# Second attention of a two-model kernel: transposes, copies and value products of a unit stand one step further behind its exponentials

## The chip, the cores and the metric

The kernel runs on one core of a Trainium2 chip. The metric is the device time of one execution in microseconds, and the text gives its median over runs. The five engines of the core each run their own instructions in order and wait for one another by semaphores: TensorE (PE, its weight loads as PEld), VectorE (DVE), ScalarE (ACT), GpSimd (POOL) and SyncE (SP, which issues transfers).

## The reference, cut to what matters

A first block (feed-forward, a mixer with a recurrence and an attention, feed-forward) is followed by a second block of two layers. The change is in the windowed attention of the second block's last layer: 16 query heads of 64 columns over 4 key heads, 512 positions in 4 blocks of 128. Each block sees its own and both neighbouring blocks (with a mask) and 256 context positions, and each head has a sink that only enters the sum.

```python
def block(bidx):
    qb = lax.dynamic_slice_in_dim(qg, start, ATT_BLOCK, axis=1)
    kb = lax.dynamic_slice_in_dim(kp, start, 3 * ATT_BLOCK, axis=1)
    vb = lax.dynamic_slice_in_dim(vp, start, 3 * ATT_BLOCK, axis=1)
    s_loc = jnp.einsum("bqkgd,bskd->bkgqs", qb, kb)
    s_loc = jnp.where(mask, s_loc, NEG_INF)
    s_ctx = jnp.einsum("bqkgd,bskd->bkgqs", qb, kc)
    p = jax.nn.softmax(jnp.concatenate([s_loc, s_ctx, s_sink], axis=-1), axis=-1)[..., :-1]
    return (jnp.einsum("bkgqs,bskd->bqkgd", p_loc, vb)
            + jnp.einsum("bkgqs,bskd->bqkgd", p_ctx, vc))
yl = jnp.moveaxis(ob, 0, 1).reshape(B, L, Q_DIM) @ w_o
```

## The kernel before

The attention is cut into 32 units (`UNITS`), each a pair of heads at one block of 128 queries, and four units make a group, which has one product with the values. `unit` gives a unit's number of key blocks: 5 (3 local and 2 of the context) for the middle two of the four query blocks, called **wide** here, and 4 for the first and the last, called **narrow**. Units 0 to 7 and 24 to 31 are narrow, 8 to 23 are wide, so of the groups 0 to 7 the groups 2 to 5 are wide.

A unit goes through these steps. The short names are used in all that follows:

- **S**, `att_scores`, PE (L694, L699): four products, local scores into banks 2 and 3, context scores into banks 0 and 1. It waits until DVE has read the scores of the unit before (`s_evac`).
- **stats**, `att_stats`, DVE (L1786 to L1794): sink column, masked copy, context copy (`s_evac` here), then the row extremum (`max_ready`).
- **E**, `att_exps`, ACT (L1242): two exponentials with their row sums, then `exp_ready`.
- **T** and **T'**, `att_turns`, PE (L715): 8 transposes into banks 4 and 5 for the block groups 0 and 1, and for a wide unit 2 more, T', for block group 2. T waits for `exp_ready` of its unit; every block group also waits until the one two before it has been copied out (`t_evac`), since there are two banks.
- **C** and **C'**, `att_copies`, ACT (L1255): the copies of those banks to `pT2`.
- For a group: **recip** on DVE (L1799), **rows** on PE (L725), the **rows copy** on ACT (L1261, `rec_copied`), **spread** on PE (L732, waits for the rows copy), the **spread copy** on ACT (L1268), **V** on PE (`att_values`, L747, 20 products of 512 columns for a wide group and 16 for a narrow one), and the **output** on DVE (`att_outputs`, L1806).

No scheduler sets the order. Each engine has a loop over U written out by hand, and what stands in a row there is run in that row; a wait holds everything behind it on that engine. One pass of such a loop is called step U here, and steps are named by U modulo 4 where that suffices: step 2 is any U with remainder 2. Before, the loops of PE and ACT are:

```
PE:  T(U-2)   S(U)     T'(U-2)  [U%4==1: rows]  [U%4==2: V, spread]
ACT: C(U-2)   E(U-1)   C'(U-2)  [U%4==2: rows copy]  [U%4==3: spread copy]
DVE: stats(U) [U%4==0: recip]   [U%4==3: output]
```

`sm2`, which holds the scores and then the exponentials, has room for four units, `pT2` for two groups. After the loops all engines but SP meet at a barrier (`phase.end`), and the projection `wo` (L524) follows.

Of the kernel before, what the change touches and what calls it, by code (L numbers as in the profile page):

```python
# [115 lines left out]
def program(nc, d):  # L116
    ctx = ExitStack()
    with ctx:
# [48 lines left out]
        def const(name):  # L167
            a, n = CONST_AT[name]
            return consts[:, a:a + n]
# [188 lines left out]
        UNITS = 4 * KT  # L358

        def unit(second, U):  # L360


            n, kv, i = U // 8, U // 4 % 2, U % 4
            lo, hi = max(n - 1, 0), (min(n + 1, LT - 1) if second else n) + 1
            return 4 * kv + i, n, kv, lo, hi, (lo - n + 1) * P, hi - lo + (2 if second else 0)

        def turned(second, U, g=0):

            return (UNITS if second else 0) + sum(-(-2 * unit(second, u)[6] // 4) for u in range(U)) + g
# [138 lines left out]
        def _(pe):  # L508
# [178 lines left out]
            def att_scores(second, U):  # L687
                x, n, kv, lo, hi, _, per = unit(second, U)
                q, k = (qt2, kt2) if second else (qk1, kt1)
                if U or second:  # L690
                    pe.wait_ge(s_evac, (UNITS if second else 0) + U)
                for s in range(2):
                    h = slice(64 * s, 64 * s + 64)
                    mm = nc.tensor.matmul(bank[2 + s][:, 0:(hi - lo) * P], q[h, x, n * P:(n + 1) * P], k[h, kv, lo * P:hi * P],  # L694
                                          start=True, stop=True)
                if second:
                    for s in range(2):
                        h = slice(64 * s, 64 * s + 64)
                        mm = nc.tensor.matmul(bank[s][:, 0:C], q[h, x, n * P:(n + 1) * P], k[h, kv, S:SC], start=True, stop=True)  # L699
                mm.then_inc(s_full, 1)  # L700

            def att_turns(second, U, gs):

                per = unit(second, U)[6]
                sm = sm2 if second else sm1
                for g in gs:
                    if 4 * g >= 2 * per:
                        continue
                    at = turned(second, U, g)
                    if g == 0:  # L710
                        pe.wait_ge(exp_ready, (UNITS if second else 0) + U + 1)
                    if at > 1:
                        pe.wait_ge(t_evac, at - 1)
                    for y in range(4 * g, min(4 * g + 4, 2 * per)):
                        tr = nc.tensor.transpose(bank[4 + at % 2][:, (y % 4) * P:(y % 4 + 1) * P],  # L715
                                                 sm[:, U % (4 if second else 3), y // per, (y % per) * P:(y % per + 1) * P], ident)
                    tr.then_inc(t_full, 1)

            def att_rows(second, G):

                N = (UNITS // 4 if second else 0) + G
                pe.wait_ge(rec_ready, N + 1)
                if N:
                    pe.wait_ge(rec_copied, 2 * N)
                nc.tensor.matmul(bank[7][0:8, 0:P], rec8[G % 2], ident, start=True, stop=True).then_inc(rec_full, 1)  # L725

            def att_spread(second, G):

                N = (UNITS // 4 if second else 0) + G
                pe.wait_ge(rec_copied, 2 * N + 1)  # L730
                for i in range(4):
                    mm = nc.tensor.matmul(bank[7][:, i * P:(i + 1) * P], const("head")[0:8, i * P:(i + 1) * P], rec_rows, start=True, stop=True)  # L732
                mm.then_inc(rec_full, 1)

            def att_values(second, G):

                U = 4 * G + 3
                x, n, kv, lo, hi, _, per = unit(second, U)
                pT, v = (pT2, v2) if second else (pT1, v1)
                G0 = UNITS // 4 if second else 0  # L740
                pe.wait_ge(t_evac, turned(second, U + 1))
                if G0 + G:
                    pe.wait_ge(o_evac, G0 + G)
                for y in range(per):
                    tile = lo + y if y < hi - lo else LT + y - (hi - lo)
                    for s in range(2):
                        mm = nc.tensor.matmul(bank[6][64 * s:64 * s + 64, :], v[:, tile, (2 * kv + s) * HD:(2 * kv + s + 1) * HD],  # L747
                                              pT[G % 2][:, s * per + y, :, :].rearrange("p i q -> p (i q)"), start=(y == 0), stop=(y == per - 1))
                mm.then_inc(o_full, 1)
# [323 lines left out]
                    pe.wait_ge(rope_free, 10 + ROTATED.index(x - ROPE_LAG) + 1)  # L1073
                    nc.tensor.matmul(bank[6][:, :], const("swap2"), HEAD_TILES[x - ROPE_LAG], start=True, stop=True).then_inc(rope_full, 1)
            phase.end()
            for U in range(UNITS + 3):
                if 0 <= U - 2 < UNITS:
                    att_turns(True, U - 2, (0, 1))
                if U < UNITS:
                    att_scores(True, U)  # L1080
                if 0 <= U - 2 < UNITS:
                    att_turns(True, U - 2, (2,))
                if U > 4 and U % 4 == 1:
                    att_rows(True, U // 4 - 1)
                if U > 4 and U % 4 == 2:
                    att_values(True, U // 4 - 1)
                    att_spread(True, U // 4 - 1)
            phase.end()
            dense("wo", 2, lambda j, k: f[:, k, :])
            phase.end()  # L1090
# [5 lines left out]
        def _(act):  # L1096
# [138 lines left out]
            def att_exps(second, U):  # L1235

                w = unit(second, U)[6] * P + 1
                sm = (sm2 if second else sm1)[:, U % (4 if second else 3), :, :]
                st = small[:, 16 * (U % 4):16 * (U % 4) + 16]
                act.wait_ge(max_ready, (UNITS if second else 0) + U + 1)  # L1240
                for s in range(2):
                    nc.scalar.activation(sm[:, s, 0:w], sm[:, s, 0:w], ACT.Exp, bias=st[:, 4 + s:5 + s], scale=-1.0,  # L1242
                                         accum_out=sums8[U // 4 % 2][:, 2 * (U % 4) + s:2 * (U % 4) + s + 1])
                act.drain().then_inc(exp_ready, 1)

            def att_copies(second, U, gs):
                per = unit(second, U)[6]
                pT = (pT2 if second else pT1)[U // 4 % 2]
                for g in gs:
                    w = min(4, 2 * per - 4 * g)  # L1250
                    if w <= 0:
                        continue
                    at = turned(second, U, g)
                    act.wait_ge(t_full, at + 1)
                    nc.scalar.activation(pT[:, 4 * g:4 * g + w, U % 4, :], bank[4 + at % 2][:, 0:w * P].rearrange("p (b q) -> p b q", b=w),  # L1255
                                         ACT.Copy).then_inc(t_evac, 1)

            def att_rows(second, G):
                N = (UNITS // 4 if second else 0) + G
                act.wait_ge(rec_full, 2 * N + 1)  # L1260
                nc.scalar.activation(rec_rows, bank[7][0:8, 0:P], ACT.Copy).then_inc(rec_copied, 1)  # L1261
# [324 lines left out]
                                     scale=1.0 / HD).then_inc(qstd_ready, 1)  # L1586
            phase.end()
            for U in range(UNITS + 4):
                if 0 <= U - 2 < UNITS:
                    att_copies(True, U - 2, (0, 1))  # L1590
                if 0 <= U - 1 < UNITS:
                    att_exps(True, U - 1)
                if 0 <= U - 2 < UNITS:
                    att_copies(True, U - 2, (2,))
                if U > 4 and U % 4 == 2:
                    att_rows(True, U // 4 - 1)
                if U > 4 and U % 4 == 3:
                    att_spread(True, U // 4 - 1)
# [8 lines left out]
        def _(dve):  # L1607
# [193 lines left out]
            def att_outputs(second, G):  # L1801
                x, n = unit(second, 4 * G)[:2]
                N = (UNITS // 4 if second else 0) + G
                dve.wait_ge(o_full, N + 1)
                dve.wait_ge(rec_copied, 2 * N + 2)
                nc.vector.tensor_tensor((f if second else qk1)[:, x:x + 4, n * P:(n + 1) * P], bank[6][:, :].rearrange("p (i q) -> p i q", i=4),  # L1806
                                        rec2 if second else rec1, ALU.mult).then_inc(o_evac, 1)
# [430 lines left out]
            phase.end()  # L2238
            nc.vector.tensor_scalar(minus_sinks, vec("sinks2"), -1.0, None, ALU.mult)
            dve.drain()  # L2240
            for U in range(UNITS + 4):
                if U < UNITS:
                    att_stats(True, U)
                if U > 0 and U % 4 == 0 and U <= UNITS:
                    att_recips(True, U // 4 - 1)
                if U > 4 and U % 4 == 3:
                    att_outputs(True, U // 4 - 1)
            phase.end()
            gated_add("wo", 1, 2, False)
            phase.end()  # L2250
# [236 lines left out]
```

## Time and profile before

| | |
|---|---|
| time before, median of 3 runs | 3304.15 us (3304.03 to 3306.55) |
| profiled execution, its own time | 3304.57 us |
| its span in the trace | 3302.8 us |
| PE matmul busy, share of the span | 2824.1 us, 86% |
| DVE busy | 1287.5 us, 39% |
| ACT busy | 803.8 us, 24% |
| the second attention, first S to the first product of `wo` | 2474.66 to 2631.30 us |
| busy in 2540 to 2560 us of it | PE 17.41, DVE 13.07, ACT 13.23 of 20 us |
| granted TensorE clock, mean of the execution | 0.928 |

The stage that is changed is 156.6 us long, 4.7% of the execution. Most of the rest is feed-forward, projections and mixture of experts, in which the change moves nothing. The share of a stage says which engine is fullest there; which wait ends last there is read from the rows of the timeline, given below.

### The profile page before, as it was taken

To read this page: it belongs to the slowest core of one execution; us is meant where nothing else is said; L and a number is where in the kernel's file an instruction comes from. 1 tells how busy PE (TensorE), PEld (TensorE's weight loads), DVE (VectorE), ACT (ScalarE), POOL (GpSimd) and SP (SyncE) were. 2 spreads that over 40 slices of the span, in tenths; PEclk is the share of its full clock that TensorE was granted. 3 is DMA by queue.
4 is the path that set the end of the run, shared out by engine and by line. 5 is a ranking of instruction groups with operands and counts; after the bars stand their busy time and mean duration, and the time that the engine had idled before them with its cause. 6 is when DMAs were issued, how large, how long until landed. Compare 5 with 4: busy or idle time off the path is not lost. (4 is left out here: it accounts for less than half of the span.)

```text
span 3302.8 us, 34854 instructions
## 1 busy us (share of the span) xinstructions
PE 2824.1 (86%) x12512; PEld 1823.7 (55%) x12512; DVE 1287.5 (39%) x1978; ACT 803.8 (24%) x1338; POOL 366.9 (11%) x484
## 2 busy tenths in 40 slices
PE   6999998999989998798868888885778887888886
PEld 4888766767768886685643333333544433333333
DVE  4776676454476755303221111113386421111112
ACT  3233235453333222222210000001326520000000
POOL 0111000000000111322101111111400001111110
PEclk9999999999999999799869898997889997999998
DMA  4666521112235665110229999995100036999997
GB/s 169 210 222 219 197 77 64 67 66 85 98 137 192 222 235 187 43 59 15 96 107 398 402 401 399 403 400 221 50 27 1 1 123 248 401 400 397 400 405 297
DMA packets 117476, 672.08 MB, mean 203 GB/s; under 512 B 16399, under 2 KB 20879, under 8 KB 51857
## 3 DMA queue, kind: packets, MB, share of 16 engines
q1 hardware_dynamic: 77456, 542.63, 42.4%
q0 software_dynamic: 33600, 104.90, 9.2%
q10 hardware_dynamic: 6336, 23.50, 2.0%
q8 instruction: 46, 0.75, 0.1%
q14 instruction: 38, 0.30, 0.0%
HBM read 672.78 MB, written 24.38 MB: 211 GB/s over the span
## 5 line engine op out<-in xcount | busy, mean ns | idle before, releaser
L823 PE MATMUL bank<-big 128*64 128x512 f32 x1040 | 479.0, 605 | 110.3 <-DMA big<-in_w 108.5
L826 PE MATMUL bank<-big 128*64 128x512 f32 x1040 | 481.4, 607 | 0.0
L1962 DVE TENSOR_TENSOR big<-big,bank 64x512 f32<-64x512 f32 x65 | 44.9, 692 | 916.3 <-ACT big L1303 916.3
L823 PEld LDWEIGHTS bank<-big 128*64 128x64 f32 x1040 | 137.7, 139 | 420.5 <-issue 418.4
L838 PE MATMUL bank<-big 128*64 128x512 f32 x1040 | 284.5, 698 | 44.4 <-DVE big L1966 44.4
L1670 DVE SCALAR_TENSOR_TENSOR tabs<-tabs,tmp 128x1024 f32<-128x1024 f32 x160 | 193.1, 1222 | 181.1 <-DMA tabs<-in_wm 180.5
L2325 POOL DMA_DIRECT2D tabs<-in_wm x160 | 85.0, 532 | 1193.0 <-DVE tabs L1670 753.6
L536 PE MATMUL bank<-act_low 128*128 128x512 f32 (+1 forms) x480 | 166.3, 363 | 48.5 <-POOL u_split L2310 25.5
L838 PEld LDWEIGHTS bank<-big 128*64 128x64 f32 x1040 | 82.6, 158 | 197.8 <-issue 196.5
L1157 ACT ACTIVATE w_high<-slot 128x1024 fp32r<-128x1024 f32 (+1 forms) x134 | 136.6, 1040 | 220.3 <-DMA slot<-in_w 94.8
L1303 ACT ACTIVATE big<-bank 64x512 f32<-64x512 f32 x65 | 38.3, 589 | 539.4 <-PE bank L823 539.4
L542 PE MATMUL bank<-u_split,w_low 128*128 128x512 f32 x656 | 162.3, 389 | 3.5 <-DVE w_low L1623 3.5
L930 PE MATMUL bank<-u_split,w_high 128*128 128x512 f32 x400 | 158.6, 396 | 0.0
L930 PE MATMUL bank<-u_low,w_high 128*128 128x512 f32 x368 | 155.2, 422 | 0.2 <-ACT w_high L1157 0.2
L1309 ACT ACTIVATE big<-bank 128x512 f32<-128x512 f32 x65 | 38.8, 597 | 457.2 <-PE bank L838 457.2
L542 PEld LDWEIGHTS bank<-u_split,w_low 128*128 128x128 f32 x656 | 123.0, 188 | 29.9 <-DVE w_low L1623 4.3
L826 PEld LDWEIGHTS bank<-big 128*64 128x64 f32 x1040 | 137.6, 139 | 0.0
L536 PE MATMUL bank<-u_split,w_high 128*128 128x512 f32 x320 | 127.1, 397 | 8.2 <-ACT w_high L1157 8.2
L536 PEld LDWEIGHTS bank<-act_low 128*128 128x128 f32 x480 | 93.6, 195 | 70.5 <-issue 24.3
L536 PE MATMUL bank<-u_split 128*128 128x512 f32 x336 | 131.6, 392 | 0.0
L536 PE MATMUL bank<-u_low,u_split 128*128 128x512 f32 x336 | 130.7, 389 | 0.0
L536 PE MATMUL bank<-u_low,w_high 128*128 128x512 f32 x320 | 126.5, 395 | 0.0
(353 smaller groups left out, 5195.1 us busy)
## 6 DMA issues: line engine op xcount, KB each, us to landing
big<-in_w SPq DMA_DIRECT2D x402, 1024.0 KB
slot<-in_w SPq DMA_DIRECT2D x100, 1024.0 KB, 4.9
tabs<-in_wm POOLq DMA_DIRECT2D x160, 512.0 KB, 4.8
slot<-in_wd SPq DMA_DIRECT2D x16, 1408.0 KB, 6.5
big<-yb ACTq DMA_DIRECT2D x20, 512.0 KB, 4.8
rows<-big ACTq DMA_DIRECT2D x10, 512.0 KB, 2.6
lat<-in_x SPq DMA_DIRECT2D x1, 2048.0 KB, 9.9
out<-lat SPq DMA_DIRECT2D x4, 512.0 KB, 3.2
```

What stands on the lines that cost most here:

```text
L536: mm = nc.tensor.matmul(out, piece[0][k], part_of[k], start=flag, stop=False)
L542: mm = nc.tensor.matmul(out, piece[1][k], high[k], start=False, stop=(last and k == n - 1))
L823: ga = nc.tensor.matmul(bank[0][lo, :], xT[:, 4 * c + k, :], wslot[c][:, k * EF:(k + 1) * EF], **flags)
L826: mm = nc.tensor.matmul(bank[0][hi, :], xT[:, 4 * c + k, :], wslot[2 + c][:, k * EF:(k + 1) * EF], **flags)
L838: mm = nc.tensor.matmul(bank[4][half, :], hT[:, 2 * c + k, :], wslot[4 + c][:, k * D + n * 512:k * D + (n + 1) * 512], start=(c == 0 and k ...
L930: mm = nc.tensor.matmul(out, wh[n // 2], (lo, hi)[n % 2][n // 2], start=(n == 0), stop=False)
L1157: nc.scalar.activation(rings[ring][:, 0:at.stop - at.start], slot[s][:, at], ACT.Copy).then_inc(wh_ready, 1)
L1303: nc.scalar.activation(hsil[MB:2 * MB, :], bank[0][0:MB, :], ACT.Silu).then_inc(q["sg_ready"], 1)
L1309: nc.scalar.activation(ysb, bank[4][:, :], ACT.Copy).then_inc(q["y_ready"], 1)
L1670: nc.vector.scalar_tensor_tensor(mslot[m % 2], mslot[m % 2], 1.0, crow, ALU.mult, ALU.mult, accum_out=modf[:, idx:idx + 1]).then_inc(mod_d ...
L1962: nc.vector.tensor_tensor(hmul[MB:2 * MB, :], hsil[MB:2 * MB, :], bank[0][MB:2 * MB, :], ALU.mult).then_inc(q["h_ready"], 1)
L2325: pool.dma_start(mslot[m % 2], d["wm"][(MOD_OF[1] + MOD_OF[2])[m] // 2]).then_inc(mod_load[m % 2], 16)
```

## The change

Every place of T, T', C and C' moves from unit U-2 to unit U-3 within the loops of PE and ACT; S, stats and E stay. V moves from step 2 to step 3, while spread stays in step 2, now with nothing between it and T'. The output moves from step 3 to the next step 0, behind recip. The loops of PE and DVE are one pass longer.

```diff
-            for U in range(UNITS + 3):
-                if 0 <= U - 2 < UNITS:
-                    att_turns(True, U - 2, (0, 1))
+            for U in range(UNITS + 4):
+                if 0 <= U - 3 < UNITS:
+                    att_turns(True, U - 3, (0, 1))
                 if U < UNITS:
                     att_scores(True, U)
-                if 0 <= U - 2 < UNITS:
-                    att_turns(True, U - 2, (2,))
+                if 0 <= U - 3 < UNITS:
+                    att_turns(True, U - 3, (2,))
                 if U > 4 and U % 4 == 1:
                     att_rows(True, U // 4 - 1)
                 if U > 4 and U % 4 == 2:
+                    att_spread(True, U // 4 - 1)
+                if U > 4 and U % 4 == 3:
                     att_values(True, U // 4 - 1)
-                    att_spread(True, U // 4 - 1)
...
-                if 0 <= U - 2 < UNITS:
-                    att_copies(True, U - 2, (0, 1))
+                if 0 <= U - 3 < UNITS:
+                    att_copies(True, U - 3, (0, 1))
                 if 0 <= U - 1 < UNITS:
                     att_exps(True, U - 1)
-                if 0 <= U - 2 < UNITS:
-                    att_copies(True, U - 2, (2,))
+                if 0 <= U - 3 < UNITS:
+                    att_copies(True, U - 3, (2,))
...
-            for U in range(UNITS + 4):
+            for U in range(UNITS + 5):
                 if U < UNITS:
                     att_stats(True, U)
                 if U > 0 and U % 4 == 0 and U <= UNITS:
                     att_recips(True, U // 4 - 1)
-                if U > 4 and U % 4 == 3:
-                    att_outputs(True, U // 4 - 1)
+                if U > 4 and U % 4 == 0:
+                    att_outputs(True, U // 4 - 2)
```

The first piece is PE's loop, the second ACT's, the third DVE's.

On PE, steps 29 to 31 and the start of what follows (narrow units), before: L725 is rows, L715 is T, L694 and L699 are S, L747 is V and L732 is spread.

```order
L725 MATMUL bank<-consts,rs 8x128
L715 MATMUL bank<-consts,big 128x128 x8
L694 MATMUL bank_3<-big 128x256 x2
L699 MATMUL bank_1<-big 128x256 x2
L747 MATMUL bank<-big 64x512 x8
L732 MATMUL bank<-rs,consts 128x128 x4
L715 MATMUL bank<-consts,big 128x128 x8
L694 MATMUL bank_3<-big 128x256 x2
L699 MATMUL bank_1<-big 128x256 x2
```

The same place of the changed kernel:

```order
L725 MATMUL bank<-consts,rs 8x128
L715 MATMUL bank<-consts,big 128x128 x8
L694 MATMUL bank_3<-big 128x256 x2
L699 MATMUL bank_1<-big 128x256 x2
L732 MATMUL bank<-rs,consts 128x128 x4
L715 MATMUL bank<-consts,big 128x128 x8
L694 MATMUL bank_3<-big 128x256 x2
L699 MATMUL bank_1<-big 128x256 x2
L747 MATMUL bank<-big 64x512 x8
```

V has gone from in front of spread to behind the next step's T and S, and spread now follows S directly.

On ACT, two wide steps around the rows copy, in the changed kernel (all line numbers are one higher there): L1256 are C' (128x2x128) and C (128x4x128), L1243 is E, L1262 the rows copy, L1269 the spread copy.

```order
L1256 ACTIVATE big<-bank 128x4x128 x2
L1243 ACTIVATE big,rs<-big,small 128x641 x2
L1256 ACTIVATE big<-bank 128x2x128
L1262 ACTIVATE rs<-bank 8x128
L1256 ACTIVATE big<-bank 128x4x128 x2
L1243 ACTIVATE big,rs<-big,small 128x641 x2
L1256 ACTIVATE big<-bank 128x2x128
L1269 ACTIVATE tmp<-bank 128x512
```

The order of kinds is that of before. What moved is which unit C and C' belong to; the rows copy still stands behind E and C' of step 2.

On DVE, around the output of a wide group, before: L1787, L1790 and L1794 are the rest of stats, L1806 is the output and L1786 begins the next stats.

```order
L1787 SCALAR_TENSOR_TENSOR big<-bank_3,consts 128x2x384
L1790 TENSOR_SCALAR big<-bank_1 128x2x256
L1794 TENSOR_REDUCE small<-big 128x2
L1806 TENSOR_TENSOR ar_f<-bank,tmp 128x4x128
L1786 COPY big<-small 128x2
```

In the changed kernel, around the output of such a group:

```order
L1791 TENSOR_SCALAR big<-bank_1 128x2x256
L1795 TENSOR_REDUCE small<-big 128x2
L1800 RECIPROCAL rs<-rs 128x8
L1807 TENSOR_TENSOR ar_f<-bank,tmp 128x4x128
L1787 COPY big<-small 128x2
```

The output has come to stand behind the reciprocal (L1800) of the next group, in step 0.

## Rows read from the trace of the kernel before

**Rows 1.** Waits in 2470:2640: engine, line waited for; us in total, times, longest

```profile
PE bank L715 <- ACTq L1244: 25.0, 24, 2.2
```

**Rows 2.** Timeline, PE, one wide group: start us, us, line, operation [idle before]

```profile
2545.01 1.12 PE L715 MATMUL bank<-consts,big 128*128 128x128 f32 x8 [0.73 <-ACTq L1244]
...
2553.77 0.92 PE L694 MATMUL bank<-big 64*128 64x384 f32 x4
...
2555.41 4.51 PE L747 MATMUL bank<-big 128*64 128x512 f32 x20
...
2559.85 1.15 PE L732 MATMUL bank<-rs,consts 8*128 8x128 f32 x8
...
2560.94 1.09 PE L715 MATMUL bank<-consts,big 128*128 128x128 f32 x8
...
2561.96 0.92 PE L694 MATMUL bank<-big 64*128 64x384 f32 x4
...
2564.41 1.12 PE L715 MATMUL bank<-consts,big 128*128 128x128 f32 x8 [0.73 <-ACTq L1244]
```

**Rows 3.** Timeline, ACT, the same group: rows copy, E, C', spread copy

```profile
2556.81 0.25 ACT L1261 ACTIVATE rs<-bank 8x128 f32<-8x128 f32 x1
...
2562.60 0.83 ACT L1242 ACTIVATE big<-big,small 128x641 f32<-128x641 f32 x1
...
2564.43 0.39 ACT L1255 ACTIVATE big<-bank 128x256 f32<-128x256 f32 x1
...
2564.71 0.59 ACT L1268 ACTIVATE tmp<-bank 128x512 f32<-128x512 f32 x1
```

**Rows 4.** Timeline, DVE, the same group: sink column, reduce, output, next sink column

```profile
2563.36 0.17 DVE L1786 COPY big<-small 128x2 f32<-128x2 f32 x1 [4.99 <-PE bank L699]
...
2565.07 1.49 DVE L1794 TENSOR_REDUCE small<-big 128x2 f32<-128x1282 f32 x1
...
2566.48 0.68 DVE L1806 TENSOR_TENSOR ar_f<-bank,tmp 128x512 f32<-128x512 f32 x1
...
2567.08 0.16 DVE L1786 COPY big<-small 128x2 f32<-128x2 f32 x1
```

**Rows 5.** Timeline, PE, one narrow group

```profile
2601.95 1.09 PE L715 MATMUL bank<-consts,big 128*128 128x128 f32 x8 [1.10 <-ACTq L1244]
...
2609.49 0.70 PE L694 MATMUL bank<-big 64*128 64x256 f32 x4
...
2610.55 3.65 PE L747 MATMUL bank<-big 128*64 128x512 f32 x16
...
2618.47 1.09 PE L715 MATMUL bank<-consts,big 128*128 128x128 f32 x8 [1.10 <-ACTq L1244]
```

**Rows 6.** Groups by shape in 2490:2628: busy us, mean ns, idle before

```profile
L1787 DVE SCALAR_TENSOR_TENSOR big<-bank,consts 128x768 f32<-128x768 f32 x16 | 15.2, 952 | 0.0
...
L1794 DVE TENSOR_REDUCE small<-big 128x2 f32<-128x1026 f32 x13 | 15.9, 1222 | 1.2
...
L1787 DVE SCALAR_TENSOR_TENSOR big<-bank,consts 128x512 f32<-128x512 f32 x13 | 8.9, 684 | 0.0
...
L1242 ACT ACTIVATE big<-big,small 128x513 f32<-128x513 f32 x27 | 19.2, 718 | 0.0
```

**Rows 7.** Timeline, the start of the stage: context copy of unit 1, S of unit 2

```profile
2481.01 0.68 DVE L1790 TENSOR_SCALAR big<-bank 128x512 f32<-128x512 f32 x1
...
2484.33 1.23 PE L694 MATMUL bank<-big 64*128 64x256 f32 x4
```

**Rows 8.** Timeline, PE, the end of the stage and the first of wo

```profile
2621.72 1.82 PE L715 MATMUL bank<-consts,big 128*128 128x128 f32 x8 [2.16 <-ACTq L1244]
...
2624.23 4.18 PE L747 MATMUL bank<-big 128*64 128x512 f32 x16 [0.16 <-ACT big L1255]
...
2631.30 10.97 PE L524 MATMUL bank<-ar_f,slot 128*128 128x512 f32 x21 [1.80 <-POOLq L355]
```

**Rows 9.** Windows: us, busy PE, PEld, DVE, ACT, POOL (count); granted clock; DMA share, GB/s

```profile
2632.50:2635.00 2.50, 2.50 (x5) 0.95 (x4) 0.00 (x0) 0.00 (x0) 0.00 (x0) 0.50 0.02 7
```

## The prediction

> **What bounds the kernel now.** I read the waits of the stage first, then the timeline of one group, and follow each engine from row to row. PE is the fullest engine of the stage, yet it waits 24 times, 25.0 us in all, for the exponentials of the unit that it is to transpose; DVE in turn waits for scores, 4.99 us behind a V [rows 1, 4]. A wide group takes 19.4 us: T starts at 2545.01, and the T four steps on at 2564.41 [rows 2]. In a step without V, T starts at 2560.94 and the next at 2564.41, 3.47 us later [rows 2]. The reader is to see that this is a closed loop: T at 2560.94, its copies, E at 2562.60, the next T at 2564.41 [rows 2, 3]. Between them ACT copies unit U-2, then does E of unit U-1, and PE needs exactly this E for its next T. The step with V is the other part: V takes from 2555.41 to 2559.85, 4.44 us, spread 1.09, and DVE then sits 4.99 us without scores [rows 2, 4]. Per wide group PE waits a few tenths to over a microsecond in each of the other three steps; 25.0 us is all that can be won if nothing else comes in.
>
> **What the change removes.** T of a unit now comes one step later, so its E was done a step before: T's wait for E goes away. The upper bound of this is the 25.0 us [rows 1]. The longer loop through DVE (S, stats, E, T, S) now spans three units and binds nothing. No operation is added or dropped but one pass of the loops; no transfer is in the stage's loops.
>
> **What is late next: the second half of T.** T's second four transposes reuse the bank of T' of the unit before, so they wait for C', and C' stands behind E on ACT. In the walk below this costs 0.7 us in step 1 and 1.0 in step 2 of a wide group (C' starts 1.83 behind E [rows 3]), between 0 and 1.0 in general, and it lies off the path that sets the end, since stats of unit 0 decides both steps. The Trainium skill (Perfetto Trace Analysis, Identifying Performance Opportunities) reads bubbles that repeat as a sign of too few buffers. It would put the remaining loss down to the two transpose banks; by my walk the sum is the same with or without that wait, and no row of before shows the wait.
>
> **What is late next: spread.** Spread waits for the rows copy on ACT. That copy stands in step 2 behind E and C'. Before, V lay in front of spread: the rows copy began at 2556.81, V had begun at 2555.41 and ran to 2559.85, so V hid the wait whole [rows 2, 3]. Now spread stands right behind T', and everything behind it on PE (T, S and V of step 3) waits with it.
>
> I walk one wide group from V to V, always along what comes last:
> - V to the T of step 0: 4.44; T to S: 1.02 (2560.94 to 2561.96) [rows 2]
> - S of unit 0 to the start of its stats: 1.40 (to 2563.36); to the reduce: 1.71 (to 2565.07) [rows 2, 4]
> - the reduce to the next DVE operation, now recip: 1.41 (2565.07 to 2566.48) [rows 4]; recip itself adds 0.1 (an estimate, between 0 and 0.2, since short operations overlap); the output, which now stands here, 0.60 (2566.48 to 2567.08) [rows 4]
> - stats of unit 1: 1.71 to its reduce, 1.49 for it, then E of unit 1: 3.20 [rows 4]
> - E to C' 1.83, C' to the next on ACT, now the rows copy, 0.28 (2562.60, 2564.43, 2564.71) [rows 3]
> - the rows copy 0.25 [rows 3] and its release 0.05 (an estimate): 0.30
> - spread 1.09, T to S 1.02, S and T' 1.64 (2553.77 to 2555.41), then V again [rows 2]
>
> Sum: 4.44 + 1.02 + 1.40 + 1.71 + 1.41 + 0.1 + 0.60 + 3.20 + 1.83 + 0.28 + 0.30 + 1.09 + 1.02 + 1.64 = 20.04 us, against 19.40: **0.65 slower**. PE would be ready for spread 1.8 us earlier (S of unit 2 can start about 8.5 behind the T of step 0, spread 1.64 later at 10.1; the rows copy is there at 11.9).
>
> The narrow group by the same walk: V shorter by 0.86 (4.51 less 3.65), S by 0.22 (0.92 less 0.70), S and T' to V 1.06 for 1.64 (2609.49 to 2610.55), two masked copies shorter by 0.27 each (952 and 684 ns), two reduces by 0.27 each (1.49 and 1222 ns), E by 0.21 (two of 0.83 and 718 ns), no C' 0.28 [rows 2 to 6]. 20.04 less 3.23 is 16.8, against 16.5 for one group (2601.95 to 2618.47 is 16.52 [rows 5]): **0.3 slower**. Its wait for the rows copy is longer, 2.1 us, since PE has less to do.
>
> **Sum over the stage, clock aside.** Eight groups go round. Three are wide throughout: 3 x 0.65 = +1.9. One is narrow throughout, +0.3. The first has no output in its step 0 and so is 0.6 shorter than a narrow one: -0.3. Two mix wide and narrow units, between 0.1 and 0.7 each: +0.8 together. The start: S of unit 2 no longer waits for the first T; it can start when unit 1's scores are read, 2481.01 + 0.68 = 2481.69, against 2484.33 [rows 7]: -2.6. The end: one step more, T without S, but spread and its copy now lie ahead of V or under it. From the T of step 32 to wo it was 2618.47 to 2631.30, 12.8 us [rows 5, 8]; the same steps in the new order come to about 11.7, and wo may start at the full clock: between -1.1 and -2.7, I take -1.5. Sum: 1.9 + 0.3 - 0.3 + 0.8 - 2.6 - 1.5 = **-1.4 us**.
>
> **The clock.** The granted clock is at its full level (2.4 GHz) in all the middle of the stage. At the end the T at 2621.72 takes 1.82 us where T takes 1.09: after 2.16 us of idle PE the clock was at its lower level (1.2 GHz) [rows 5, 8]. The first products of wo, after 1.80 us idle, ran low too, with a granted clock of 0.50 in 2632.5 to 2635 [rows 8, 9]. The V behind the first of these took 4.18 against 3.65 [rows 5, 8], so one fall costs 0.73 + 0.53 and a few tenths for the S between: 1.5 us. Idle of 1.10 in a step did not lower it [rows 5]. The new wait for the rows copy is 2.1 us in the groups with narrow E, three of them, with 0.4 idle shortly before, and 1.7 to 1.8 in wide ones. The first is as long as the one that lowered the clock, the second just short of the other. I take three falls, +4.5; the ends are none, 0, and eight, +12. With it the forecast is -1.4 + 4.5 = **+3.1 us**. The profiled execution's own time is 3304.57, so 3307.7 on it; it lies 0.4 above the median of 3304.15, and on the median I say **3307.3**.
>
> **The rivals.**
> - *Slower, by the clock.* If the wide groups' waits of 1.7 to 1.8 us lower the clock as well, spread, T, S and V run low behind each wait, and all of them lie on the path. Eight falls: -1.4 + 12 = +10.6, 3314.8. It decides at five falls (+6.1), about where a difference can be told. For it: 1.80 did it before wo. Against: in a wide group T' and the split T leave PE busier just before.
> - *Quicker, the wait is covered.* If the rows copy were there when PE comes to spread, the wide walk would end with S of unit 2 at 8.5, then 1.64 + 1.09 + 1.02 + 1.64 + 4.44: 18.3, 1.1 less than before, and a narrow group 14.7, 1.8 less. Three wide, two mixed at 1.5, three narrow: -3.3 - 3.0 - 5.4, with start and end -4.1: -15.8, 3288. For it speaks only that the waited-for E goes; against it that the rows copy stood behind E and C' at 2556.81, 1.4 us behind the point at which spread would now be issued [rows 2, 3]. The Trainium skill (Perfetto Trace Analysis, Identifying the Most-Contended Engine) takes weight-load time, not matmul time, for how near TensorE is to its limit; by that PE has room and most of the 25.0 us could come back, 3279 at best. The rows speak against it: from start to start PE's own work fills all but about 2.6 of 19.4 us of a wide group.
> - *The clock never falls.* The waits for the rows copy stay too short, and start and end weigh against the eight groups: -1.4, 3302.8.
>
> **How the numbers follow.** Forecast (the wait for the rows copy shows, two to four falls) 0.47; no or one fall 0.18, 3302.8 to 3304; five or more falls 0.24, 3310 to 3317; wait covered 0.08, 3288; something on PE that no row shows, 0.03 to either side. A measurement of this kernel can tell about 0.2%, 6.6 us. Faster by more than that (below 3297.5): the covered case and the odd one, 0.10. Slower (above 3310.8): 0.24 of falls less the part that stays below, plus the odd one, 0.23. Within: 0.67. The range leaves out the covered case (0.08), the odd ones and the top of the falls: 3300 to 3315.
>
> **What would show it.** A wait of PE at L733 (spread) for ACT's rows copy (L1262), 8 times, 1.7 to 2.2 us each, some 15 us in all, where before had none. PE's wait for exponentials at T falls from 25.0 us to under 5, and waits at the second half of T for C' come up in the wide groups. A wide group of 20.0 us and a narrow one of 16.8. DVE's wait for scores about as before. Spreads of 1.5 to 2 us instead of 1.15, and T of 1.8, where the clock fell. The forecast is wrong if spread shows no wait, if a wide group is below 19 us, or if the clock is low behind each wide group's wait.

## The result, and the profile after

The changed kernel takes 3320.1 us (median of 6 runs, 3318.7 to 3320.9), the kernel before 3304.1 in 6 runs beside it: a ratio of 1.0045, 95% interval 1.0033 to 1.0057. It is 0.45% or 15 us slower by the ratio, which goes by all runs; the two medians lie 16 us apart. The forecast was 3307.3 with a range of 3300 to 3315, so the time lies outside the range, on the side of the rival that goes by the clock. Another set of runs gave 1.0039 (1.0025 to 1.0053).

The profiled execution after has a span of 3317.7 us, 14.9 more than before. From the first S of the second attention to the first product of `wo` it takes 169.3 us (2475.18 to 2644.50) against 156.6. `wo` itself is 1.7 us shorter, since it now starts at the full clock. What is ahead of the stage differs by 0.5 us and what is behind `wo` by 3.4, in work that the change leaves alone.

The waits of PE in the stage, in the changed kernel (engine, line waited for; us in total, times, longest; lines of PE's helpers keep their numbers, so spread is L732, where the prediction wrote L733, and T is L715; lines behind the loops are one higher than before, so L1262 is the rows copy, L1256 C and C', L1791 the context copy of stats):

```profile
PE bank L732 <- ACT rs L1262: 13.5, 8, 2.4
PE bank L715 <- ACT big L1256: 6.4, 9, 1.0
PE bank L694 <- DVE big L1791: 6.0, 8, 1.5
...
PE bank L725 <- DVE rs L1800: 1.6, 3, 1.0
```

The 25.0 us that PE waited for exponentials [rows 1] are gone without a rest. In their place stand 13.5 us at spread, eight times, 6.4 us at the second half of T, 6.0 for the reading of scores and 1.6 at rows: 27.5 us, only 2.5 more than those 25.0. That alone is no 15 us.

One wide group in which the clock stays up, PE (start us, us, line, operation, idle before):

```profile
2551.21 1.09 PE L715 MATMUL bank<-consts,big 128*128 128x128 f32 x8
...
2555.14 0.66 PE L715 MATMUL bank<-consts,big 128*128 128x128 f32 x4 [0.76 <-ACT big L1256]
...
2563.06 1.15 PE L732 MATMUL bank<-rs,consts 8*128 8x128 f32 x8 [1.62 <-ACT rs L1262]
...
2566.82 4.51 PE L747 MATMUL bank<-big 128*64 128x512 f32 x20
...
2571.26 1.09 PE L715 MATMUL bank<-consts,big 128*128 128x128 f32 x8
```

and in the same group ACT, with the weight loads of spread (PEld):

```profile
2562.48 0.38 ACT L1256 ACTIVATE big<-bank 128x256 f32<-128x256 f32 x1
2562.76 0.25 ACT L1262 ACTIVATE rs<-bank 8x128 f32<-8x128 f32 x1
2563.06 0.96 PEld L732 LDWEIGHTS bank<-rs,consts 8*128 8x128 f32 x8 [1.85 <-ACT rs L1262]
```

From T to T it is 20.05 us, where the walk of the prediction gave 20.04 and before had 19.40 [rows 2]. The rows copy begins 0.28 behind C' and spread 0.30 behind its begin, to the hundredth what was summed up. DVE goes from the reduce of unit 0 through recip and output to the stats of unit 1 without waiting:

```profile
2555.34 1.49 DVE L1795 TENSOR_REDUCE small<-big 128x2 f32<-128x1282 f32 x1
2556.75 0.19 DVE L1800 RECIPROCAL rs<-rs 128x8 f32<-128x8 f32 x1
2556.86 0.64 DVE L1807 TENSOR_TENSOR ar_f<-bank,tmp 128x512 f32<-128x512 f32 x1
2557.41 0.16 DVE L1787 COPY big<-small 128x2 f32<-128x2 f32 x1
```

PE had the scores of unit 1 ready at 2557.07, ahead of the stats at 2557.41, though the second half of T at 2555.14 had waited 0.76 us for C': that wait is off the path, as the walk had it.

Now the narrow group at the end, PE:

```profile
2611.22 1.09 PE L715 MATMUL bank<-consts,big 128*128 128x128 f32 x8
...
2618.09 0.70 PE L694 MATMUL bank<-big 64*128 64x256 f32 x4 [0.41 <-DVE big L1791]
...
2621.32 2.07 PE L732 MATMUL bank<-rs,consts 8*128 8x128 f32 x8 [2.10 <-ACT rs L1262]
2623.32 1.97 PE L715 MATMUL bank<-consts,big 128*128 128x128 f32 x8
2625.22 1.23 PE L694 MATMUL bank<-big 64*128 64x256 f32 x4
...
2627.22 3.87 PE L747 MATMUL bank<-big 128*64 128x512 f32 x16
2631.03 1.09 PE L715 MATMUL bank<-consts,big 128*128 128x128 f32 x8
```

Up to spread it follows the walk. Then spread takes 2.00 us to the next T instead of 1.09, T 1.90 to S instead of 1.02, S 2.00 to V instead of 1.06: 2.7 us lost in the three, and 0.2 in V. The group takes 19.81 us against 16.52 before [rows 5] and 16.8 in the walk.

The granted clock in stretches of the changed kernel (us; busy PE, PEld, DVE, ACT, POOL; granted clock; DMA share, GB/s):

```profile
2518.70:2525.30 6.60, 5.78 (x24) 4.53 (x24) 1.66 (x2) 3.04 (x8) 0.00 (x0) 0.50 0.00 0
2542.30:2545.70 3.40, 3.40 (x15) 2.51 (x15) 0.40 (x1) 1.70 (x3) 0.00 (x0) 0.51 0.02 5
2556.00:2572.00 16.00, 13.59 (x83) 7.24 (x82) 10.74 (x15) 9.52 (x23) 0.00 (x0) 1.00 0.00 1
...
2621.00:2627.40 6.40, 6.08 (x26) 4.70 (x28) 1.00 (x2) 2.87 (x7) 0.00 (x0) 0.50 0.00 0
```

A stretch at the lower level (1.2 GHz) is called a fall of the clock here. Five of the eight waits at spread have one that begins in the wait or within 2 us behind it, 3.4 us long at two of them and 6.8 at three, and a sixth fall, of 3.4 us, begins just ahead of the last V. From 14 us into the stage on, before had a single one, of 3.4 us, in the T at 2621.72 [rows 8].

### The profile page after: what moved, and what is told of

It is laid out like the page before. It is cut to its first block and busy times, and to the rows that moved or that the text cites. A ratio compares the mean times of both kernels' runs of the same rounds, so it can differ in the third digit from the quotient of the medians.

```text
span 3317.7 us, 34854 instructions
## 1 busy us (share of the span) xinstructions
PE 2838.2 (86%) x12512; PEld 1832.1 (55%) x12512; DVE 1287.0 (39%) x1978; ACT 803.9 (24%) x1338; POOL 366.2 (11%) x484
```

## The experiments

Theory A: the wait for the rows copy, uncovered at spread, costs a little by itself and most through the clock that falls behind it. Theory B: the deeper lag costs, by its additional step and the split T. The table sums up all runs; each ratio is to the kernel before in the same set of runs. "Wide" is the time from S of unit 16 to S of unit 20, "narrow" from S of unit 4 to S of unit 8 (ahead of the first output), "low" the time at the lower clock in the stage, its first 16 us left out. Stage, wide, narrow and low come from one profiled execution of each kernel.

| kernel | ratio (95% interval) | stage, us | wide | narrow | low |
|---|---|---|---|---|---|
| before | 1 | 156.6 | 19.40 | 16.58 | 3.4 |
| changed | 1.0045 (1.0033 to 1.0057) | 169.3 | 20.05 | 19.43 | 31 |
| changed, again | 1.0039 (1.0025 to 1.0053) | 173.2 | 20.05 | 19.45 | 37 |
| e1, spread behind V | 0.9968 (0.9954 to 0.9982) | 148.3 | 19.47 | 14.70 | 0.8 |
| e2, rows copy first | 0.9948 (0.9928 to 0.9968) | 143.9 | 18.39 | 14.57 | 3.4 |
| e3, lag of two, spread uncovered | 1.0031 (1.0018 to 1.0043) | 172.3 | 23.20 | 16.86 | 31 |
| e4, four fillers | 1.0029 (1.0020 to 1.0039) | 169.5 | 21.94 | 17.78 | 0 |
| e5, two fillers | 0.9994 (0.9985 to 1.0004) | 156.8 | 20.22 | 16.26 | 0 |
| e6, e2 and C' first | 0.9966 (0.9952 to 0.9979) | 143.0 | 17.72 | 14.57 | 6.8 |
| e7, e2 and output in step 1 | 0.9957 (0.9944 to 0.9971) | 143.5 | 18.37 | 14.57 | 3.4 |
| e8, e3 and rows copy first | 0.9980 (0.9971 to 0.9990) | 150.3 | 18.38 | 15.58 | 6.8 |
| e9, e6 and e7 | 0.9956 (0.9942 to 0.9970) | 140.7 | 17.58 | 14.57 | 3.4 |
| e10, e9 and fillers at the end | 0.9947 (0.9934 to 0.9959) | 139.1 | 17.58 | 14.57 | 0 |

Times of the whole kernel scatter by some 5 us up and down in these sets (before: 3299.6 to 3312.0). In the traces much of that lies outside the stage: its first S comes between 2469.0 and 2477.7 us, and from the first product of `wo` to the end it takes 670.7 to 679.1. So the stage's own length shows more than the ratios do, as long as the falls in it are looked at too: the changed kernel's two executions differ by 3.9 us there, by their falls. (In the second, two records of the first S are missing; its start is set from the spacing of the next ones.)

**e1, spread covered by V again.**

```diff
-                if U > 4 and U % 4 == 2:
-                    att_spread(True, U // 4 - 1)
                 if U > 4 and U % 4 == 3:
                     att_values(True, U // 4 - 1)
+                    att_spread(True, U // 4 - 1)
```

> The changed kernel with spread moved behind V in step 3; the lag of three stays. Theory A (the uncovered wait for the rows copy, and the clock that falls behind it, make the change slower): PE waits no more at spread, the clock falls no more in the middle of the stage, a wide group takes about 19.4 us (V 4.44 and spread 1.09 as before, but the second half of T waits for C'), a narrow one about 15.2, the stage about 149 us against 156.6 before: 3296 us. Theory B (the deeper lag costs by itself, through one more step and the split T): the time stays near the changed kernel's 3320.

Waits of PE in the stage in e1:

```profile
PE bank L715 <- ACT big L1255: 10.2, 13, 1.0
PE bank L694 <- DVE big L1790: 7.6, 11, 1.5
```

No wait at spread, no fall of the clock but 0.8 us at the very end, a wide group of 19.47 us and a stage of 148.3: theory A's numbers (19.4 and 149); a narrow group takes 14.70 where 15.2 was expected. B falls: with the lag of three in full, the kernel is 0.3% faster than before. In wide groups the lag gains nothing this way; what PE no longer waits for E, it waits for C' (10.2 us).

**e2, the rows copy ahead of E.**

```diff
+                if U > 4 and U % 4 == 2:
+                    att_rows(True, U // 4 - 1)
                 if 0 <= U - 1 < UNITS:
                     att_exps(True, U - 1)
                 if 0 <= U - 3 < UNITS:
                     att_copies(True, U - 3, (2,))
-                if U > 4 and U % 4 == 2:
-                    att_rows(True, U // 4 - 1)
```

> The changed kernel with the rows copy of ACT moved ahead of E in step 2; PE's order is untouched. Theory A: spread finds the rows copy done, a wide group takes 18.3 us and a narrow one 14.7, no falls of the clock, stage about 142 us: 3290 us. Theory B: only the 13.5 us of waits at spread go at best, the falls stay: 3306 or more.

One wide group of e2, PE:

```profile
2547.28 0.44 PE L715 MATMUL bank<-consts,big 128*128 128x128 f32 x2
2547.64 1.15 PE L732 MATMUL bank<-rs,consts 8*128 8x128 f32 x8
2548.73 1.12 PE L715 MATMUL bank<-consts,big 128*128 128x128 f32 x8
...
2551.42 4.51 PE L747 MATMUL bank<-big 128*64 128x512 f32 x20
2555.86 1.09 PE L715 MATMUL bank<-consts,big 128*128 128x128 f32 x8
```

Spread follows T' by 0.36 us, without a wait, and PE runs from there through V without a gap. 18.39 us a wide group (18.3 expected), 14.57 a narrow one (14.7). "No falls" did not come true: one of 3.4 us is left in the last V, and the stage takes 143.9 us for 142. One ACT operation of 0.25 us, moved ahead of E, turns 0.45% slower into 0.52% faster. This is the rival "the wait is covered" of the prediction, made true.

**e3, the uncovered spread without the lag.** The kernel before, with V, spread and output where the change has them, T and C left at U-2:

```diff
                 if U > 4 and U % 4 == 2:
-                    att_values(True, U // 4 - 1)
                     att_spread(True, U // 4 - 1)
+                if U > 4 and U % 4 == 3:
+                    att_values(True, U // 4 - 1)
...
-                if U > 4 and U % 4 == 3:
-                    att_outputs(True, U // 4 - 1)
+                if U > 4 and U % 4 == 0:
+                    att_outputs(True, U // 4 - 2)
```

> The kernel before (lag of two) with only V, spread and the output placed as in the change: spread right behind T' in step 2, V in step 3, output in step 0. Theory A: spread waits 1.4 to 1.5 us for the rows copy in every group, a wide group takes 20.0 us and a narrow one 16.9; 3305 without a fall of the clock, up to 3315 with a fall in each narrow group. Theory B: placing spread there is harmless at any lag, 3304.

Its waits, and one low stretch of a wide group:

```profile
PE bank L715 <- ACTq L1245: 18.4, 17, 2.2
PE bank L732 <- ACT rs L1262: 11.2, 8, 1.6
```

```profile
2562.40:2569.00 6.60, 6.60 (x27) 4.27 (x27) 1.85 (x4) 3.20 (x8) 0.00 (x0) 0.51 0.00 0
```

It is slow without any deeper lag, by 0.31%, with 11.2 us of waits at spread and 31 us at the lower clock. The mechanism of A is confirmed. By the ratio the 10 us lie within what was expected (up to 11 with falls), but the profiled execution is among the slower ones and its stage is 15.7 us longer than before's: I had expected falls in narrow groups only, and all three wide groups have one (21.6, 23.2 and 21.7 us for a walk of 20.0), after waits of 1.6 us at most, while the first group, after a wait of 1.44, has none.

**e4 and e5, work in place of the wait.** Products of constants into the idle bank 6 ahead of each spread, four in e4 and two in e5. Each shows as two records in the trace, as every product here but the transposes does: the x20 of a wide V are 10 products of the program, the x16 of a narrow one 8. The edit of e5:

```diff
                 if U > 4 and U % 4 == 2:
+                    N = UNITS // 4 + U // 4 - 1
+                    pe.wait_ge(o_evac, N)
+                    for _ in range(2):
+                        nc.tensor.matmul(bank[6][0:64, :], consts[:, 0:64], consts[:, 0:512], start=True, stop=True)
                     att_spread(True, U // 4 - 1)
```

> The changed kernel with four products of 512 columns of constants into the idle bank 6 just ahead of each spread (1.7 us of PE work in the place of the wait; results unused). Theory A in its clock part: the granted clock stays at its full level through the stage, the spreads are 1.15 us again, and the 12 us that I read as lost to the clock come back: 3308 us, though PE does 14 us more work. If the falls are a side effect and the waits alone cost: 3320 or more.

> As e4_fillers, with two products in place of four: e4's four took 3.6 us ahead of each spread, longer than the wait that they replace (1.6 to 2.4 us), so its time held both effects; two take 1.8 us (results unused). If the falls of the clock make up the rest of the slowdown, no fall is left in the stage, a wide group stays at 20.05 us, a narrow one at 17, the stage takes 157 us against 169.3 of the changed kernel and the time equals before's, ratio 1.000. If the waits alone cost, it stays 0.3% or more above.

The narrow group of e5 that answers to the one shown of the changed kernel, PE (L1089 are the fillers):

```profile
2608.91 1.93 PE L1089 MATMUL bank<-consts 128*64 128x512 f32 x4
2611.08 1.15 PE L732 MATMUL bank<-rs,consts 8*128 8x128 f32 x8 [0.24 <-ACT rs L1266]
2612.16 1.09 PE L715 MATMUL bank<-consts,big 128*128 128x128 f32 x8
...
2614.25 3.65 PE L747 MATMUL bank<-big 128*64 128x512 f32 x16
2617.83 1.09 PE L715 MATMUL bank<-consts,big 128*128 128x128 f32 x8
```

e4 was badly sized: its fillers took 3.6 us, twice the wait, so that it stays slow at the full clock and tells the two theories of its expectation apart only together with e5. e5 fits: spread starts about when it did in the changed kernel, but is 1.15 us long again and T 1.09. No fall is left, the stage takes 156.8 us, 157 had been expected, and the ratio is 1 within its interval. Taking the falls away shortens the stage by 12.5 us, nearly all of the 12.7 by which it had grown. It is not quite what they cost. The fillers occupy 1.8 us, longer than the wait in five of the groups (by 0.2 in each of the three wide ones, which is why they take 20.22 us for 20.05; by 0.5 in the sixth group and 0.9 in the last), 1.9 us in all. And the first four units take 0.8 us less in e5 (13.58 for 14.35), because the low stretch that comes in from ahead of the stage ended earlier in that execution. So the falls cost about 12.5 + 1.9 - 0.8 = 13.6 us, an estimate from these rows, more than the whole growth.

**e6, C' ahead of E as well; e7, the output in step 1; e9, both.** In e6 ACT does C, the rows copy, C', E. In e7 and e9 DVE has:

```diff
-                if U > 4 and U % 4 == 0:
+                if U > 5 and U % 4 == 1:
                     att_outputs(True, U // 4 - 2)
```

> e2 with, in addition, C' of ACT ahead of E, so that the second half of T finds its bank free. If those waits (6.4 us in e2) are on the path, a wide group falls from 18.4 to about 17.7 us and the stage from 143.9 to 141: 0.1% below e2. If E, later by the wait for T', takes their place, no change or a loss against e2.

> e2 with, in addition, the output of DVE in step 1, behind stats instead of ahead of it. By my walk the output's 0.6 us lies on the path from stats of unit 0 to S of unit 2 in every group: 0.5 less per narrow group, 0.6 per wide one where C' does not bind, stage about 140. If it is off the path: 143.9 as e2.

> e6 and e7 together: rows copy and C' ahead of E, output in step 1. With the waits for C' gone, a wide group should be bound by the reading of the scores, and the output's 0.6 us then lies on that path: 17.1 us against 17.7 in e6, two microseconds over the stage. If PE's own 16.6 to 16.8 us a group or a wait that I don't see binds, it stays at 17.7.

e6 gives wide groups of 17.72 us, as expected, yet the stage is only 0.9 us shorter than e2's: its last step runs low for 6.8 us instead of 3.4, which takes back 1.5 of the 2.4 us won. e7 is a miss: 18.37 against 18.39 in a wide group and 143.5 in the stage; only the second group, from S of unit 8 to S of unit 12, gains (16.22 for 16.49). In wide groups the output is off the path, since S there waits for the second half of T (6.4 us of such waits in e7 as in e2). In e9 the wide group is 17.58, not 17.1: PE's own work (16.6) and a microsecond in short stops of 0.15 to 0.3 us ahead of T', spread and one S are what is left. By the ratios e2, e7, e9 and e10 can't be told apart.

**e8, the lag of two with the rows copy first.** e3 with the edit of e2.

> e3 (lag of two, spread right behind T', V in step 3) with the rows copy ahead of E. Theory A as it stands now: the wait at spread goes, a wide group takes 18.4 us, as with the lag of three, a narrow one 15.7 (14.7 with three), stage 148 against 156.6 before: 0.25% faster than before, so that most of the gain of e2 comes from the place of spread and rows copy and about 4 us from the lag. If the lag is what matters: near before's time, 156.

```profile
PE bank L715 <- ACTq L1245: 19.2, 20, 2.2
...
PE bank L732 <- ACT rs L1262: 0.4, 1, 0.4
```

A wide group takes 18.38 us, the same as e2's with the lag of three; a narrow one 15.58, a microsecond more. PE still waits 19.2 us for exponentials, and it matters only in the narrow groups and at the start: the stage is 150.3 against e2's 143.9. So splitting V from spread and covering the rows copy gains 6.4 us of stage, and the lag of three as much again, none of it in a wide group: 3.2 us at the start, 1.0 in each of the first two groups that follow, 1.3 at the end, where e8's fall is 6.8 us long and e2's 3.4 (what decides that is open). The 148 us that had been expected were 2 too few.

**e10, fillers at the end.** e9 with one product of constants in each of steps 33 and 34, into bank 0:

```diff
+                if U in (UNITS + 1, UNITS + 2):
+                    pe.wait_ge(s_evac, 2 * UNITS)
+                    nc.tensor.matmul(bank[0][0:64, :], consts[:, 0:64], consts[:, 0:512], start=True, stop=True)
                 if U > 4 and U % 4 == 1:
                     att_rows(True, U // 4 - 1)
```

> e9 with one product of constants into bank 0 (results unused) in each of steps 33 and 34, where PE waits 1.0 us for the last reciprocal and 0.9 us for the last rows copy. If the fall of the clock at the end of the stage comes from that idle time, the last spread and V run at the full clock: the stretch from the last S to wo goes from 19.6 to about 16.5 us and the stage gets 3 us shorter. If not, it gets up to 1 us longer.

The end of the stage in e2 and in e10, PE (L1085 are the fillers):

```profile
2611.85 1.26 PE L732 MATMUL bank<-rs,consts 8*128 8x128 f32 x8 [0.88 <-ACT rs L1262]
2613.04 5.20 PE L747 MATMUL bank<-big 128*64 128x512 f32 x16
```

```profile
2608.33 1.07 PE L1085 MATMUL bank<-consts 128*64 128x512 f32 x2
2609.33 1.15 PE L732 MATMUL bank<-rs,consts 8*128 8x128 f32 x8
2610.41 3.65 PE L747 MATMUL bank<-big 128*64 128x512 f32 x16
```

The fall at the end is gone, as expected if it comes from the idle time there. From the last S to `wo` it takes 16.5 us, against 18.1 in e9 and 19.65 in e6, and the stage is 1.6 us shorter than e9's: half of what was expected, since e9 itself had one short low stretch and not e6's long one. With 139.1 us it is the shortest stage of all, 17.6 us below before, and 0.53% faster over the kernel.

**The changed kernel again.**

> The changed kernel itself once more, beside the same runs of the kernel before as the experiments: a ratio of 1.0045 again, within 0.0015, with the same six falls of the clock in the trace if the falls follow from the order of the work, or other groups if they depend on chance.

Its ratio is 1.0039, within the 0.0015 expected. The waits are the same to the tenth (13.5 us at spread), the falls are not: seven of them, the new one in the wide group of units 20 to 23, which took 20.05 us in the first execution and 23.20 in this one. The narrow groups have theirs both times. So neither answer of the expectation holds whole: the same six recur, and a seventh comes at the same waits.

## Why the prediction was wrong

- **Right: what goes and what comes.** T's wait for E went to nothing, the wait at spread came eight times (13.5 us; "some 15" had been said), the second half of T waits for C' off the path that sets the end. DVE's wait for scores, said to stay "about as before", went from 46.9 to 56.7 us; without the falls, in e5, it is 45.1.
- **Right in the groups, too cautious at the end: the walk.** A wide group without a fall takes 20.05 us (20.04), and the first, the wide and the mixed groups come out within a tenth. The sum without the clock had been -1.4 us up to the end of `wo`. e5, which keeps the waits and takes away the falls, comes to 212.0 us from the first S to the end of `wo` against 213.5 before, -1.5, but that agreement is luck: its fillers cost 1.9 and its start is 0.8 shorter than the changed kernel's. Without both the sum is about -2.7: the start gave 2.8 us for 2.6 taken, the last narrow group and the end together 2.4 for 1.2.
- **Wrong: the clock, the term of three falls at 1.5 us.** Both factors were too small. The count: five falls in the groups and one in the last V, and seven in another execution, where three were taken. Wide groups fall too, one of three and in the other execution two, after waits of 1.6 us, and the sixth group after one of 1.30, which I had put on the safe side because 1.80 and 2.16 were the idle times ahead of the two falls in the rows [rows 8]. The price: the fall at 2621.72 of before had cost 1.5 us. In the changed kernel three last 6.8 us, twice as long, and cost 2.7 to 3.2 each (the last narrow group 19.81 for 16.8); the 3.4 us ones cost 1.6 (a wide group 21.64 for 20.05). The six add up to 13.7 us where 4.5 stood (e5 gives 13.6).
- **How the whole comes out.** Of the 11.8 us by which the profiled execution exceeds its forecast of +3.1, the falls are 9.2 and what lies outside the stage and `wo` 3.9; the walk takes 1.3 back.
- **What could have been seen.** The trace of before has both factors outside the stage. At 1840.30 us a stretch of 3.3 us at the lower clock begins in an idle time of only 0.69 us (one of 1.41 lay seven us earlier), and one of 6.8 us begins at 2413.75, 61 us ahead of the stage, in 3.24 us of idle. PE and the granted clock there, in the kernel before (formats as above; the 16 records at the full clock take 3.65 us [rows 5], here 5.26):

```profile
1840.40 5.26 PE L838 MATMUL bank<-big 128*64 128x512 f32 x16 [0.69 <-DVE big L1966]
...
2414.85 2.04 PE L1074 MATMUL bank<-big,consts 128*128 128x512 f32 x2 [3.24 <-DVE rs L1812]
```

```profile
1840.30:1843.60 3.30, 3.20 (x8) 1.03 (x10) 0.00 (x0) 0.00 (x0) 0.55 (x1) 0.50 1.01 420
2413.75:2420.55 6.80, 5.70 (x21) 4.70 (x22) 6.39 (x7) 0.00 (x0) 0.00 (x0) 0.50 0.00 0
```

- **The rival.** "Slower, by the clock" had this mechanism, with eight falls at 1.5 and a chance of 0.24, and its top of 3317 still lies below the result, since it carried the same price. The range took the count from 0 to 8 and the price as known, from one fall, and bounded it from one side only.
- What stays open: why the same wait brings a fall in one group and none in the next. Also the profiled execution has 3.4 us more behind `wo` and 0.5 ahead of the stage. Other kernels show differences of that size there in both directions, and no experiment was made on it.

## What to carry to other kernels

A wait that no row of the trace shows may be hidden by the work that stands ahead of it on the waiting engine; whoever moves that work has to look for what each instruction behind it waits for, and for what stands ahead of the releaser on the other engine. Idle time on TensorE can have a second price, the half-speed stretch behind it: look for such stretches in the whole trace, not in the changed stage alone, and for count and price take a range, not the one fall that the stage happens to hold. Moving a quarter-microsecond copy ahead of two long exponentials took the changed kernel's stage from 169.3 to 143.9 us; of the 12.8 us that this is below before, half came without the deeper pipeline (e8) and half with it.

## What the runs showed of the hardware

At spread the clock fell at waits of 1.3 to 2.4 us, and whether a given wait of 1.6 us did it differed from group to group and from one execution to the next at the same waits. In the last steps it fell behind two shorter stops, 1.00 and 0.88 us, with a T between them; filled with products (e10), they brought no fall. Falls in the stage lasted 3.4 us or twice that, and cost 1.6 us or 2.7 to 3.2. In them eight transposes took 1.97 us against 1.09. PE work of no use in the gaps, 14 us in all in e5, bought 12.5 us back.
